# Down projection of a hybrid decoder layer: one set of activation sums for both halves, six Strassen places in each, and a smaller software DMA scratch

## What is computed

```python
x = x + merged @ w_out[i]
h2 = rms_norm(x, ln_ffn_w[i])
u = causal_depthwise_conv(h2 @ w_up[i], conv_w[i], conv_b[i])
u_gate, u_val = jnp.split(u, 2, axis=-1)
x = x + (jax.nn.silu(u_gate) * u_val) @ w_down[i]          # the down projection
h3 = rms_norm(x, ln_ple_w[i])
x = x + jax.nn.sigmoid(h3 @ w_ple_gate[i]) * (p[i] @ w_ple[i])
```

## Time and profile before

| | |
|---|---|
| median of 3 runs | 1422.74 us (1422.71 to 1422.91) |
| profiled execution, its own time | 1423.26 us |
| its span, first to last instruction | 1421.5 us |
| instructions | 19857 |
| TensorE matmul busy | 1411.3 us, 99% |
| VectorE busy | 1088.8 us, 77% |
| ScalarE busy | 793.7 us, 56% |
| mean granted TensorE clock | 0.999 |

### The profile page before, as it was taken

The page is one execution under the profiler, slowest core; times in us unless marked ns, Lnnn a source line. Parts: engine busy times, 40 slices in busy tenths (PEclk is TensorE's granted clock), DMA queues, the critical chain, the costliest instruction groups (busy, mean ns, idle before and its releaser), DMA issues.

```text
span 1421.5 us, 19857 instructions
## 1 busy us (share of the span) xinstructions
PE 1411.3 (99%) x7054; PEld 1199.0 (84%) x7054; DVE 1088.8 (77%) x1386; ACT 793.7 (56%) x965; POOL 133.5 (9%) x87
## 2 busy tenths in 40 slices
PE   9999999999999999999999999999999999999997
PEld 7888888888888888888888888888888888888886
DVE  7676767878787888777777777777777888888887
ACT  7565665555455555465555555555555555554654
POOL 0024124100000000001110101101011000000000
PEclk9999999999999999999999999999999999999999
DMA  9655565565665665475656566566665565565663
GB/s 321 204 179 162 162 192 150 162 186 177 201 204 186 219 237 197 157 222 179 194 178 198 185 189 192 177 196 186 192 192 178 199 201 198 173 209 205 215 221 120
DMA packets 190733, 273.48 MB, mean 192 GB/s; under 512 B 11728, under 2 KB 103120, under 8 KB 190544
## 3 DMA queue, kind: packets, MB, share of 16 engines
q1 hardware_dynamic: 190096, 272.04, 59.8%
q10 hardware_dynamic: 576, 0.63, 0.1%
HBM read 270.53 MB, written 2.10 MB: 192 GB/s over the span
## 4 chain that ended last, share of the span: by engine, by line
PE 98%; DVE 1%; DMA 0%; ACT 0%; issue 0%; DVEq 0%; ACTq 0%
PE aux L996 11%; PE main L996 11%; PE main L744 9%; PE main L745 9%; PE main L746 9%; PE aux L1005 6%; PE main L802 6%; PE main L803 6%; PE main L804 6%; PE main L1005 6%; PE aux L802 4%; PE aux L804 4%; PE aux L803 4%; PE aux L745 2%; PE aux L744 2%; PE aux L746 2%
## 5 line engine op out<-in xcount | busy, mean ns | idle before, releaser
L1638 DVE TENSOR_TENSOR w_lo<-raw,w_hi 128x1024 fp32r<-128x1024 f32 (+1 forms) x476 | 581.1, 1235 | 272.4 <-ACT w_hi L1304 271.6
L1304 ACT ACTIVATE w_hi<-raw 128x1024 fp32r<-128x1024 f32 (+1 forms) x476 | 499.4, 1051 | 453.6 <-PE main L746 100.3
L744 PE MATMUL main<-w_hi,xT 128*128 128x512 f32 x446 | 175.8, 394 | 0.3 <-DVE w_lo L2215 0.3
L745 PE MATMUL main<-w_lo,xT 128*128 128x512 f32 x446 | 173.7, 389 | 0.0
L746 PE MATMUL main<-w_hi,xT 128*128 128x512 f32 x446 | 173.6, 389 | 0.0
L996 PE MATMUL aux<-xT,w_hi 128*128 128x512 f32 x704 | 169.7, 391 | 0.0
L996 PE MATMUL main<-xT,w_hi 128*128 128x512 f32 x672 | 162.8, 391 | 0.0
L996 PEld LDWEIGHTS aux<-xT,w_hi 128*128 128x128 f32 x704 | 129.4, 188 | 25.0
L996 PEld LDWEIGHTS main<-xT,w_hi 128*128 128x128 f32 x672 | 123.2, 188 | 23.6
L2340 POOL TENSOR_TENSOR act<-cv 128x512 f32<-128x512 f32 (+1 forms) x22 | 71.8, 3266 | 418.5 <-DVE cv L1880 418.5
L744 PEld LDWEIGHTS main<-w_hi,xT 128*128 128x128 f32 x446 | 83.8, 188 | 17.7 <-DVE xT L1665 1.2
(11 more groups left out here) (381 smaller groups left out, 2250.2 us busy)
## 6 DMA issues: line engine op xcount, KB each, us to landing
raw<-in_w_up SPq DMA_DIRECT2D x336, 256.0 KB
raw<-in_w_in SPq DMA_DIRECT2D x136, 512.0 KB
raw<-in_w_down SPq DMA_DIRECT2D x84, 512.0 KB
raw<-in_w_out SPq DMA_DIRECT2D x32, 512.0 KB
raw<-in_w_ple_gate SPq DMA_DIRECT2D x32, 512.0 KB
raw<-in_w_branch_a SPq DMA_DIRECT2D x16, 512.0 KB
raw<-in_w_branch_b SPq DMA_DIRECT2D x16, 512.0 KB
raw<-in_w_in SPq DMA_DIRECT2D x15, 256.0 KB, 5.8
```

Of the source, the lines that this page charges most:

```text
L744: pe.matmul(acc, th, wh, start=first, stop=False)
L745: pe.matmul(acc, th, wl, start=False, stop=False)
L1304: ac.activation(w_hi[:, u % RING, :, 0:w], raw[:, u % RING, :, 0:w], ACT.Copy).then_inc(hi_full, 1)
L1638: dve.tensor_tensor(w_lo[:, u % RING, :, 0:w], raw[:, u % RING, :, 0:w], w_hi[:, u % RING, :, 0:w].bitcast(F32), ALU.subtract).then_inc(lo ...
```

## The change

- `SEVEN_AT`: from five places in each half, at row tile pairs 5, 8, 11, 14, 17, to six in each half, at 5, 8, 10, 13, 15, 17. In units, the first half's places begin at 394, 400, 404, 410, 414, 418 instead of 394, 400, 406, 412, 418; the second half's are the same numbers plus 44.
- `FORM`, `SUMS_AT`: the down projection has six forms instead of ten. The second half's places use the forms that the first half made at the same row tile pairs; no forms are made for the second half. By the rule of due times, the first half's forms are due at slots 392, 396, 400, 406, 410, 414 (before: 392, 396, 402, 408, 414).
- Four of the six forms get buffers of their own, `more_sums_hi` and `more_sums_lo`, 16 KB per partition together, so that they stay until the second half has used them.
- `dynamic_dma_scratch_size=1024` and `FILL` from 312 to 56 free that room: 15 KB of the scratch that is set aside for DMAs whose descriptors software writes, and 1 KB of an unused filler tile.

```diff
-SEVEN_AT = ((5, 8, 11, 14, 17), (5, 8, 11, 14, 17))
+SEVEN_AT = ((5, 8, 10, 13, 15, 17),) * 2
...
-        + [DOWN_FORMS + q for q in range(len(SEVENS) - N_GATES - N_OUTS)])
+        + [DOWN_FORMS + SEVEN_AT[p].index(i) for p in range(2) for i in SEVEN_AT[p]]
+        + [DOWN_FORMS + len(SEVEN_AT[0]) + f for f in range(len(LAST_AT))])
...
-SUMS_AT.update((max(u - 4, DOWN + UK), FORM[q]) for u, q in SEVEN.items() if DOWN <= u < GATE)
+SUMS_AT.update((max(u - 4, DOWN + UK), FORM[q]) for u, q in SEVEN.items() if DOWN <= u < DOWN + 2 * UD)
...
-FILL = 312
+FILL = 56
...
+        more_sums_hi = sb("more_sums_hi", [P, 4, 4, P], F32R, ffn)
+        more_sums_lo = sb("more_sums_lo", [P, 4, 4, P], F32R, ffn)
...
         def form_place(f):
+            if DOWN_FORMS + 2 <= f < N_FORMS - len(LAST_AT):
+                return f - DOWN_FORMS + 1
             return 2 if f == 2 else f % 2
...
-            return a_sums_hi[:, f % 2], a_sums_lo[:, f % 2]
+            if form_place(f) > 2:
+                return more_sums_hi[:, form_place(f) - 3], more_sums_lo[:, form_place(f) - 3]
+            return a_sums_hi[:, form_place(f)], a_sums_lo[:, form_place(f)]
...
-            return max(e for e in range(f) if form_place(e) == form_place(f))
+            return max((e for e in range(f) if form_place(e) == form_place(f)), default=None)
...
-                    if q >= len(GATES_AT):
+                    if form_before(q) is not None:
                         ac.wait_ge(w_sums_done, 2 * max(r + 1 for r in range(len(SEVENS)) if FORM[r] == form_before(q)))
...
-                    u = SEVENS[FORM.index(f)]
-                    k, hi, lo = u - DOWN - 2 * UD * (u >= DOWN + 2 * UD), aT_hi, aT_lo
+                    k, hi, lo = 2 * SEVEN_AT[0][f - DOWN_FORMS], aT_hi, aT_lo
...
-    nc = bacc.Bacc("TRN2", target_bir_lowering=False, num_devices=1)
+    nc = bacc.Bacc("TRN2", target_bir_lowering=False, num_devices=1, dynamic_dma_scratch_size=1024)
```

## The result

The median of 20 runs is 1425.61 us (1424.81 to 1427.42), beside 1423.03 us (1422.71 to 1423.46) for the kernel before in the same comparison: a ratio of 1.0019, 95% interval 1.0012 to 1.0026. That is +2.6 us, where +2.2 was forecast from a median of 1422.74. The profiled execution took 1425.36 us, its span is 1423.6 us; against 1423.26 and 1421.5 that is +2.1 us by either. The median of 1425.61 lies at the upper end of the forecast's own range, 1424.0 to 1425.6, which was counted from a median for the kernel before that is 0.29 lower than the one here.

The account below looks back on a forecast made before the run. TensorE was taken to bound the kernel, with VectorE able to come late. Waits 1.0 + 1.1 + 1.2, restarts 0.25, less 1.36 saved, gave +2.2 us: median 1424.9 us, own range 1424.0 to 1425.6, with rivals 1421.3 to 1427.0.

Parts of the forecast that it names:

- The saved matmuls: Down projection: two more places save three matmuls each of 0.2267 us on TensorE's path, 1.36 us together.
- The three waits: First half, places 400, 410, 414: TensorE waits on low weight sums behind the moved form, 1.0, 1.1 and 1.2 us.
- The restart: After each first-half wait the matmul behind the released one starts 0.31 us later, not 0.23: 0.08 each, 0.25 for three.
- the order: VectorE in slots 400, 410, 414: a form of 1.90 us goes ahead of weight sums that have 0.90 us of room.
- the other number of the working: First half, period of four units: VectorE has 11.4 us of work against 10.20 us on TensorE.
- idle time of VectorE elsewhere: Place 400: VectorE's 1.76 us idle before 1133.90 does not shorten the wait, which hangs on TensorE's end of unit 399.
- The waits did come: Rival, chance 0.15: no waits at the first half's weight sums, only the saved matmuls count, 1421.4 us.
- VectorE as the bound of the whole half: Rival, chance 0.14: units 400 to 422, VectorE also late for low parts of units 406, 412, 416, 420; 1427.0 us.
- The late loads: First half: loads behind the weight differences slip past VectorE's 0.6 to 0.9 us lead; a 0.6 us slip decides.
- The pace of the matmuls: Rival, chance 0.08: moved tensors change the pace by one nanosecond on 7054 matmuls, 7 us either way, 1416 or 1430.

Follow-up runs that it names:

- e2_order: The changed kernel with VectorE running the form behind the low part of the weight sums in slots 400, 410 and 414: 1425.03 us, ratio 1.0015.
- e5_one_pair: The changed kernel with five places in each half, at pairs 5, 8, 10, 14, 17, so one close pair instead of three: 1424.03 us, ratio 1.0007.
- e6_places_only: The kernel before with only the list of places changed to six per half, every place making its own form: 1429.03 us, ratio 1.0045.
- e8_change_again: The changed kernel itself, timed again beside the others on the same chip: 1425.53 us, ratio 1.0017.
- e1_reuse_only: The changed kernel with five places per half at the old pairs; shared forms and smaller scratch stay: 1422.98 us, ratio 1.0000.
- e7_second_six: The changed kernel with the old five places in the first half, six in the second, three forms made early where VectorE idles: 1422.35 us, ratio 0.9995.
- e4_pool_forms: The changed kernel with join and sums of five down projection forms on GpSimd instead of VectorE: 1428.08 us, ratio 1.0037.

## Why the prediction was right

**The saved matmuls.** The second half, from its first matmul to that of the gate stage, went from 115.35 us (1199.15 to 1314.50) to 114.67 (1201.84 to 1316.51): 0.68 less, the three matmuls of one place, and no wait there, as costed. The first matmuls of the two stages, before and after:

```profile
1199.15 0.39 PE L802 MATMUL aux<-w_hi,aT_hi 128*128 128x512 f32 x1
...
1314.50 0.39 PE L744 MATMUL main<-w_hi,xT 128*128 128x512 f32 x1
```

```profile
1201.84 0.39 PE L809 MATMUL aux<-w_hi,aT_hi 128*128 128x512 f32 x1
...
1316.51 0.39 PE L751 MATMUL main<-w_hi,xT 128*128 128x512 f32 x1
```

**The three waits.** They came at the places, on the line and behind the instructions that were named: 0.91, 1.26 and 0.99, 3.16 us, for 1.0, 1.1 and 1.2, 3.3. The first was 0.09 shorter than worked out, because TensorE starts 0.05 us after the end of the weight sums (1133.67 to 1133.72), not the 0.14 that was read at unit 396. The restart was 0.11 and not 0.08, since the matmul behind a wait on weight sums starts 0.34 us later, not 0.31. With 3.16 + 0.33 - 1.36 the sum is +2.13; the profiled execution shows +2.1. That the two agree so closely is partly luck. The first half, from its first matmul to that of the second, grew by 3.09 us (114.18 to 117.27), where these terms give 3.16 + 0.33 - 0.68 = 2.81 and the prediction named 2.9; the rest is in small steps, such as matmuls behind the waits that start 0.24 us apart. Against it, the first half began 0.40 us earlier than in the profile of the kernel before (1084.57, 1084.97). Over the ten profiles it begins between 1084.50 and 1084.97; what moves it is open.

**The reason given for them was half of it.** The working put the weight on the order: a form in front of what TensorE waits for. That says where the wait shows up. `e2_order` shows that turning the order round only moves it, and that the other number of the working, 11.4 us of VectorE in a period of 10.2 us of TensorE, is what costs. The statement that idle time of VectorE elsewhere does not shorten the wait was meant for place 400, which hangs on TensorE's end of unit 399, and holds there (0.91 in all four profiles with a form in slot 400: the change, `e5_one_pair`, `e6_places_only`, `e8_change_again`). At 410 the wait hangs on something else. VectorE idles some 2 us there until the load of unit 408, the fifth from the start of place 404, has come and been rounded, and then works 14.42 us without a pause up to the weight sums that TensorE waits for. It resumes 11.65, 11.45 and 11.27 us after TensorE's first released matmul at 402 (the change, `e8_change_again`, first half of `e6_places_only`), and the wait at 410 is 1.26, 1.15 and 0.99. So the second wait has the right size for a reason that is only half in the working: too much work, counted from a late load.

**The median.** It rose by 2.6 where the profile has 2.1. The runs of the change lie between 1424.81 and 1427.42, those of before within 0.75 us. The larger part of this scatter lies outside the spans: those of the 20 runs, first to last instruction, lie between 1423.0 and 1424.2 us, with a median of 1423.4, some 2.2 above the 1421.2 of the kernel before in the first comparison of the experiments. What lies around the span is 1.74 to 4.22 us; the run of 1427.42 us has a span of 1423.2. The sum forecasts the span and came out right there. What the median rose beyond that lies around the span, and no run here shows what makes it. Within the span, the second wait follows the load, as above.

**The rivals.** The waits did come, at all three places. VectorE as the bound of the whole half did not: low parts of units 406 to 420 cause no wait in the change. The late loads on which that rival rested do show, in the size of the second wait. The pace of the matmuls did not move with the tensors (`e1_reuse_only`: the second half takes 115.34 us beside 115.35).

## What to carry to other kernels

On an engine that paces itself a little ahead of the busiest one, sum its work per period before packing the period denser: 11.4 us into 10.2, 1.2 too much, cost 0.7 to 1.3 us each time, whichever of the two orders was used. Saving three matmuls of 0.23 us was worth it only where the side work had room (`e7_second_six`, 0.8 us by the medians), not where it had none. Sharing work that is off the path earns nothing by itself; it pays when it makes room for something.

## What the runs showed of the hardware

GpSimd and VectorE hindered each other when both ran additions and subtractions with two inputs in SBUF. In `e4_pool_forms` a VectorE subtraction of 128x1024 that began 0.39 us behind a join on GpSimd took 2.31 us in place of 1.22, and that join took 1.61. A join that began 0.22 us behind a VectorE subtraction (1135.86, 1135.64) took 2.14 us, and the subtraction kept its 1.22; the next one on VectorE, of 128x512, then took 1.78 us in place of 0.69. The Trainium skill (SBUF — State Buffer, "SBUF: two separate sides") says that a VectorE operation with two SBUF inputs and a GpSimd operation that reads SBUF share a pair of ports, which whoever starts first holds; these rows agree, in that the one that began first kept the shorter time. Not every row does: in the up stage of the same run a GpSimd product that began 0.16 us behind two low parts on VectorE (1053.21, 1053.05) took 3.35 us, and neither low part got longer (2.35 us for both); why is open. The main line of that expectation had taken an idle engine for a free one.
